# Attention probabilities turned by VectorE in 32x32 blocks and moved through DRAM instead of by TensorE

## The chip, the cores and the metric

The kernel runs on one core of one Trainium2 chip. The metric is the device time in microseconds (us) of the whole kernel, the median of several executions. The engines are TensorE (PE), VectorE (DVE), ScalarE (ACT), GpSimd (POOL) and SyncE (SP); SP, POOL and ACT issue the transfers, which 16 DMA engines carry out.

## What is computed

Two layers over 256 latent tokens and 256 context tokens of width 1024, all in float32. Cut to what matters here, a layer is

```
h, hc = modulate(rms_norm(x)), modulate(rms_norm(ctx))         # adaLN
a_b, a_c, a_x, na_q, na_k, na_v, sw_q, sw_k, sw_v, gates = split(h @ w_in)
o_a  = a_b * short_conv(a_c * a_x)                             # branch 0
o_na = neighbourhood_attention(na_q, na_k, na_v, context k, v, bias)   # branch 1, 8 heads of 64
o_sw = window_attention(sw_q, sw_k, sw_v, context k, v, sink)          # branch 2, 8 heads of 64
merged = sum_i sigmoid(gate_i) * (o_i @ w_branch[i])
x += gate * (merged @ w_out)
x += gate * expert_choice_ffn(h2)     # 16 experts, 1024 x 1024 gate, up, down
```

An attention is `softmax(q k^T + bias) v` over 512 keys (latent and context) for a latent query and over 256 context keys for a context query. The second layer has latent queries only, because the context is not needed after it.

## The kernel before

`make_plan` writes one list of steps for all engines; each engine walks the list and takes the steps that concern it, so that every engine's order is that list's order and semaphores tie the engines together. Around the attention the list is made of **pairs**. A pair is the two heads of one head pair `p` (0 to 3) for one tile of 128 queries. In layer one each `p` has four pairs: latent queries tile 0 (512 keys), context tile 0 (256 keys), latent tile 1, context tile 1. In layer two it has two, both with 512 keys. Over the two branches that is 32 pairs in layer one and 16 in layer two. A **set** is the pairs of one `p` that share a product with the values: two pairs.

`attention(br, p, info, fill)` places for each pair: the step `score` (TensorE makes both heads' scores into two PSUM banks, VectorE adds the bias and finds the maximum, ScalarE writes `PB = exp(scores)`), then a share of the filling blocks (`fill`: the products of the next `p`'s queries and keys, of gates and branches), and among them `normalise` for each head (VectorE: `PB *= 1/sum`, L1758). Behind the share stands `turn`: TensorE transposes each 128x128 piece of `PB` into a PSUM bank (L2058), ScalarE copies the bank to `PTL` or `PTC` (L1452). The step `pv` of a set (TensorE, L2071) stands in the next pair's filling; `o_low` follows it. So queries' probabilities are used as the moving operand of the value product about a third of a pair after they were turned.

A filling block is the product of a 128-column weight block with `HH`/`HL` or `OH`/`OL`, three matmuls for each of its 8 (or 4) row tiles (L2019 to L2021, "k steps"). Its weights come by SP's queue into a stretch of `ring` (`P.load`, two slots of 4096 words in layer one and three in layer two, used round and round), ScalarE rounds them to `WH` (L1362) and VectorE writes the rest `WL` (L1598), two blocks ahead of TensorE, with three buffers.

POOL serves the bias of the neighbourhood attention: for each unit (one head of one pair) two transfers from DRAM into `BIAS` (L1256) and an addition of the mask (L1227). SP waits at the step `gt2_bias` for the last value product of the layer (`pv_ready`) before it issues what stands behind it, the next dense weights and, in layer two, the first expert weights. The mixture of experts behind it streams 16 experts' weights through the ring.

## Time and profile before

| | us |
|---|---|
| median of 3 executions | 1842.83 (1837.32 to 1845.15) |
| the profiled execution, its own time | 1841.04 |
| its span in the profile | 1838.9 |
| TensorE, VectorE, ScalarE, GpSimd busy | 1690.3, 771.2, 478.1, 111.1 |

In the profiled execution layer one's attention lies from about 150 to 412 us, its experts from about 590 to 1070 us, layer two's attention from about 1123 to 1306 us, its experts from about 1396 us to the end. Times of instructions are read from such a profile with `PE` for matmuls and `PEld` for loads of the stationary operand; matmuls overlap, so that the distance between starts, and not the duration of one, is what one costs in a row of them.

### The profile page before, as it was taken

The numbers are of one execution on the slowest core, as the hardware profiler recorded it, in microseconds if no ns is written. First come the engines' busy times: TensorE is split into PE (matmuls) and PEld (weight loads), VectorE is DVE, ScalarE is ACT, GpSimd is POOL, SyncE is SP. The second block draws the span as 40 slices with busy tenths as digits, with TensorE's granted clock in tenths as the row PEclk, the third lists the DMA queues.
The fourth block names the chain that finished last, engine by engine and source line by source line (L and its number), as shares of the span: only waits on it lengthen the run. The fifth ranks groups of instructions, "written<-read, shape, count | busy, mean of one in ns | idle before, by whom it ended". The sixth has DMA issues, their size and how long they took to land.

```text
span 1838.9 us, 26514 instructions
## 1 busy us (share of the span) xinstructions
PE 1690.3 (92%) x10854; PEld 979.8 (53%) x10854; DVE 771.2 (42%) x1746; ACT 478.1 (26%) x1052; POOL 111.1 (6%) x149
## 2 busy tenths in 40 slices
PE   6999999999998999999988799989998998777876
PEld 3887777776664333333232498877882332222222
DVE  4455566665424233332323665577753222111111
ACT  4224455552132100000000434465441000000001
POOL 1012210000001000000000102300001000000000
PEclk9999999999998999999999899999999999999899
DMA  9353231127778999999999764337899999999997
GB/s 352 112 137 95 84 92 58 36 80 264 268 275 343 410 428 426 428 428 427 427 428 427 264 203 141 89 115 256 282 365 383 426 427 426 426 426 426 425 426 298
DMA packets 152035, 543.83 MB, mean 296 GB/s; under 512 B 10026, under 2 KB 92400, under 8 KB 126700
## 3 DMA queue, kind: packets, MB, share of 16 engines
q1 hardware_dynamic: 149104, 535.35, 74.2%
q0 software_dynamic: 2400, 6.16, 1.3%
q8 instruction: 87, 1.43, 0.3%
q10 hardware_dynamic: 412, 0.64, 0.1%
q14 instruction: 32, 0.26, 0.0%
HBM read 539.13 MB, written 2.98 MB: 295 GB/s over the span
## 4 chain that ended last, share of the span: by engine, by line
PE 69%; DMA 23%; DVE 4%; ACT 2%; issue 1%; SPq 1%; POOL 0%; DVEq 0%; ACTq 0%
PE bank L2158 20%; PE bank L2019 12%; PE bank L2020 11%; PE bank L2021 11%; DMA ring<-in_w_exp_down 8%; DMA ring<-in_w_exp_gate 7%; DMA ring<-in_w_exp_up 5%; DMA spare<-in_w_exp_gate 3%; PE bank L1934 2%; PE bank L2132 2%; PE bank L2048 2%; PE bank L2071 2%; PE bank L2058 2%; PE bank L2187 1%; DMA ring<-in_w_in 1%
## 5 line engine op out<-in xcount | busy, mean ns | idle before, releaser
L2158 PE MATMUL bank<-ring,XEP 128*32 128x256 f32 (+1 forms) x2384 | 385.3, 618 | 30.5 <-DMA ring<-in_w_exp_gate 15.2
L2019 PE MATMUL bank<-HH,WH 128*128 128x512 f32 (+1 forms) x864 | 312.2, 361 | 4.2 <-DVE HL L1627 3.1
L2020 PE MATMUL bank<-HL,WH 128*128 128x512 f32 (+1 forms) x864 | 300.5, 348 | 0.0
L2021 PE MATMUL bank<-HH,WL 128*128 128x512 f32 (+1 forms) x864 | 300.0, 347 | 0.0
L2158 PEld LDWEIGHTS bank<-ring,XEP 128*32 128x32 f32 (+1 forms) x2384 | 114.4, 130 | 271.2 <-issue 228.4
L1598 DVE TENSOR_TENSOR WL<-ring,WH 128x1024 fp32r<-128x1024 f32 (+1 forms) x172 | 185.2, 1079 | 133.6 <-ACT WH L1362 132.9
L1856 DVE TENSOR_TENSOR X<-X,bank 128x512 f32<-128x512 f32 x184 | 114.0, 682 | 186.5 <-PE bank L2187 99.4
L2019 PEld LDWEIGHTS bank<-HH,WH 128*128 128x128 f32 x864 | 164.0, 190 | 52.1 <-issue 24.5
L1362 ACT CAST WH<-ring 128x1024 fp32r<-128x1024 f32 (+1 forms) x172 | 158.1, 927 | 101.2 <-PE bank L2021 64.7
L2158 PE MATMUL bank<-ring,HIDT 128*32 128x256 f32 (+1 forms) x1232 | 151.6, 474 | 32.1 <-DMA ring<-in_w_exp_down 32.1
L2021 PEld LDWEIGHTS bank<-HH,WL 128*128 128x128 f32 x864 | 164.0, 190 | 21.0
L2020 PEld LDWEIGHTS bank<-HL,WH 128*128 128x128 f32 x864 | 164.3, 190 | 18.2
L2158 PEld LDWEIGHTS bank<-ring,HIDT 128*32 128x32 f32 (+1 forms) x1232 | 55.9, 123 | 110.8 <-issue 72.9
L1506 ACT ACTIVATE HIDT<-bank 128x512 f32<-128x512 f32 (+1 forms) x32 | 15.7, 490 | 371.7 <-PE bank L2220 371.7
L1891 DVE TENSOR_TENSOR HID<-TH,bank 128x512 f32<-128x512 f32 (+1 forms) x32 | 17.8, 555 | 211.7 <-issue 203.5
L1842 DVE TENSOR_TENSOR YE<-bank,GT 128x512 f32<-128x512 f32 (+1 forms) x32 | 17.9, 558 | 207.0 <-PE bank L2158 207.0
L1500 ACT ACTIVATE TH<-bank 128x512 f32<-128x512 f32 (+1 forms) x32 | 15.7, 490 | 284.3 <-PE bank L2158 284.3
L2019 PE MATMUL bank<-OH,WH 128*128 128x512 f32 (+1 forms) x192 | 67.8, 353 | 1.6 <-issue 0.8
L1284 POOL TENSOR_TENSOR XEP<-XEP,MOD 128x512 f32<-128x512 f32 (+1 forms) x32 | 25.8, 828 | 664.8 <-DVE XEP L1834 664.8
L2020 PE MATMUL bank<-OL,WH 128*128 128x512 f32 (+1 forms) x192 | 64.9, 338 | 0.0
L2021 PE MATMUL bank<-OH,WL 128*128 128x512 f32 (+1 forms) x192 | 64.7, 337 | 0.0
L1256 POOL DMA_DIRECT2D BIAS<-rpb_tiled x64 | 39.4, 620 | 327.0 <-DVE SM L1734 204.2
(244 smaller groups left out, 1961.5 us busy)
## 6 DMA issues: line engine op xcount, KB each, us to landing
ring<-in_w_exp_gate SPq DMA_DIRECT2D x55, 2048.0 KB, 31.1
ring<-in_w_exp_up SPq DMA_DIRECT2D x49, 2048.0 KB, 33.9
ring<-in_w_exp_down SPq DMA_DIRECT2D x48, 2048.0 KB, 35.7
ring<-in_w_ada SPq DMA_DIRECT2D x48, 1024.0 KB, 7.6
ring<-in_w_in SPq DMA_DIRECT2D x40, 1024.0 KB, 6.2
split_slot<-in_w_exp_up SPq DMA_DIRECT2D x8, 2048.0 KB, 28.9
split_slot<-in_w_exp_down SPq DMA_DIRECT2D x8, 2048.0 KB, 33.3
ring<-in_w_in SPq DMA_DIRECT2D x28, 512.0 KB, 5.4
```

Source lines behind the costliest of these rows:

```text
L1256: pool.dma_start(BIAS[x.at][64 * rr:64 * rr + 64, :].rearrange("p (r k) -> p r k", r=4), toeplitz).then_inc(bias_in[x.bias % 2], 16)
L1362: nc.scalar.copy(WH[b.buffer][:, 0:b.kk, :], w).then_inc(split_hi, 1)
L1598: nc.vector.tensor_tensor(WL[b.buffer][:, 0:b.kk, :], w, WH[b.buffer][:, 0:b.kk, :].bitcast(f32), ALU.subtract).then_inc(split_lo, 1)
L1856: nc.vector.tensor_tensor(xs, xs, ys, ALU.add).then_inc(x_added, 1)
L1934: last = mm(t[32 * j:32 * j + 32, :], CS[:, 4 * kk + j, :], w[:, j, :], start=kk == 0, stop=kk == 1, tile_position=(0, 32 * j))
L2019: mm(t, wh, hi[:, k, 0:b.n], start=k == 0, stop=False)
L2020: mm(t, wh, lo[:, k, 0:b.n], start=False, stop=False)
L2021: last = mm(t, wl, hi[:, k, 0:b.n], start=False, stop=k == b.kk - 1)
L2048: last = mm(SB_[x.u % 2][:, 0:x.nk], QS[x.p % 2][rows, qp, q0:q0 + 128], k, start=i == 0, stop=i == 2, tile_position=(64 * x.hh, 0))
L2058: last = nc.tensor.transpose(TB[x.u % 2][:, 128 * c:128 * c + 128], PB[x.u % 2][:, 128 * c:128 * c + 128], IDENT)
L2071: last = mm(PVB[64 * hh:64 * hh + 64, 0:SEQ], v, buf[:, hh, c, :], start=c == 0, stop=c == n - 1, tile_position=(0, 64 * hh))
L2158: last = mm(out_bank[tw * g:tw * g + tw, 0:nw], stationary(k), w[:, g::G] if spread else w[:, nw * g:nw * g + nw], start=k == 0, stop=k == ...
```

## The change

VectorE transposes each unit's `PB` in 32x32 blocks into `PBT`, right behind its normalisation. When both heads of a pair are there, POOL writes `PBT` to one of three DRAM tensors (`bounce`), and with four transfers reads it back so that block (i, j) lands at (j, i) in `PTL` or `PTC`. TensorE's transposes and ScalarE's copies are gone. In layer one the read-back is issued behind the next pair's write; in layer two right behind its own. The value product of a set is placed three pairs (layer one) or two pairs (layer two) behind the pair that ends it. `PBT` takes the last 1024 words of the streaming stretch of `ring` (`P.kept`). The bias transfers are placed by `bias_order` behind a pair's write, the two masks behind the four transfers. `gates_first` puts two gate blocks ahead of the branch blocks where a branch's values come late. The last sets of a layer are multiplied inside the first filling of branch 2.

```diff
@@ class Plan.load
-            if self.top + size > STREAM[self.layer] * SLOT:
+            if self.top + size > STREAM[self.layer] * SLOT - self.kept:
@@ attention
-                at_ = sorted(at_ + [(-(-per * 3 // 10), values), (-(-per * 7 // 10), lower)], key=lambda a: a[0])
+                at_ = sorted(at_ + [(-(-per * ((1 if br == 'sw' and p == 0 else 5) if last else 4) // 10), lambda: values(pair[0].pair - (2 if last else 3))), (-(-per * ((4 if br == 'sw' and p == 0 else 10) if last else 8) // 10), lower)], key=lambda a: a[0])
-        def values():
-
-            for st in P.turned:
-                P.add("pv", set=st)
-            P.lower += P.turned
-            P.turned = []
+        def values(until):
+
+            while P.turned and P.turned[0].end <= until + 1:
+                P.add("pv", set=P.turned[0])
+                P.lower.append(P.turned.pop(0))
@@ def turn(pair)
-            for x in pair:
-                P.add("turn", unit=x)
-                if x.end:
-                    P.turned.append(x.set)
+            P.add("turn", pair=pair)
+            P.fetches.append(pair)
+            if last or len(P.fetches) > 1:
+                P.add("fetch", pair=P.fetches.pop(0))
+            if pair[1].end:
+                P.turned.append(pair[1].set)
@@ branch 2, the first filling
+            if d2 == 0:
+                mid = 2 * KD + 3
+                atoms = gates_first(atoms)
+                done = 0
+                for n in (KD + 1, 2 * KD)[-len(P.turned):]:
+                    run(atoms[done:n])
+                    values(P.turned[0].end - 1)
+                    run(atoms[n:n + 3])
+                    lower()
+                    done = n + 3
+                run(atoms[done:mid])
@@ gpsimd
+                    elif s.kind == "turn":
+                        x = s.pair[1]
+                        pool.wait_ge(turn_ready, x.u + 1)
+                        run, held = 16 * x.nk // 32, bounce[x.pair % 3]
+                        if x.pair > 2:
+                            pool.wait_ge(pt_in[x.pair % 3], 64 * (x.pair // 3))
+                        pool.dma_start(held[:, 0:4 * run], PBT[l][x.set.grp][:].rearrange("p b h c j -> p (b h c j)")).then_inc(pt_out, 16)
+                    elif s.kind == "fetch":
+                        x = s.pair[1]
+                        run, held = 16 * x.nk // 32, bounce[x.pair % 3]
+                        pool.wait_ge(pt_out, 16 * (x.pair + 1))
+                        if x.set.pt_before:
+                            pool.wait_ge(pv_ready, x.set.pt_before)
+                        j = x.qt % 2
+                        for b in range(4):
+                            blocks = bass.AP(tensor=held.tensor, offset=held.offset + run * b, ap=[[PBT_W, 32], [32 * PBT_W, 4], [1, run]])
+                            turned = (PTL, PTC)[x.set.grp][32 * b:32 * b + 32, 4 * j:4 * j + 4].rearrange("p a h c j -> p a (h c j)")
+                            pool.dma_start(turned, blocks).then_inc(pt_in[x.pair % 3], 16)
@@ scalar, kind == "turn": the copy is gone
-                        nc.scalar.copy(buf[:, x.hh, :, 128 * j:128 * j + 128],
-                                       TB[x.u % 2][:, 0:128 * nk].rearrange("p (k q) -> p k q", k=nk)).then_inc(pt_ready, 1)
@@ vector, kind == "normalise"
+                        dve.wait_ge(norm_ready, x.u + 1)
+                        if x.hh == 0 and x.pair:
+                            dve.wait_ge(pt_out, 16 * x.pair)
+                        turned = PBT[l][x.set.grp][:, :, x.hh, :, :].rearrange("p b c j -> p c b j")
+                        nc.vector.transpose(turned, PB[u2][:, 0:n].rearrange("p (c b j) -> p c b j", b=4, j=32)).then_inc(turn_ready, 1)
@@ tensor, kind == "turn": the transposes are gone
-                        for c in range(x.nk // 128):
-                            last = nc.tensor.transpose(TB[x.u % 2][:, 128 * c:128 * c + 128], PB[x.u % 2][:, 128 * c:128 * c + 128], IDENT)
@@ tensor, kind == "pv"
-                        pe.wait_ge(pt_ready, st.end)
+                        for n in st.pairs:
+                            pe.wait_ge(pt_in[n % 3], 64 * (n // 3 + 1))
```

VectorE, first pair of layer one, before: the two heads' normalisations stand one behind the other, then a weight block's `WL`.

```order
L1750 TENSOR_TENSOR SM<-SM 128x1 [waits exp_ready]
L1757 RECIPROCAL SM<-SM 128x1 [waits dve_chain]
L1758 TENSOR_SCALAR PB_90<-PB_90,SM 128x512 [waits dve_chain]
...
L1758 TENSOR_SCALAR PB_91<-PB_91,SM 128x512 [waits dve_chain]
L1598 TENSOR_TENSOR WL_83<-ring,WH_80 128x1024 [waits split_hi]
```

The same place of the changed kernel:

```order
L1804 TENSOR_SCALAR PB_94<-PB_94,SM 128x512 [waits dve_chain]
L1809 STREAM_TRANSPOSE PBT_90<-PB_94 128x4x4x32 [waits norm_ready]
...
L1804 TENSOR_SCALAR PB_95<-PB_95,SM 128x512 [waits dve_chain]
L1809 STREAM_TRANSPOSE PBT_90<-PB_95 128x4x4x32 [waits norm_ready]
L1650 TENSOR_TENSOR WL_83<-ring,WH_80 128x1024 [waits split_hi]
```

A transpose of the unit's whole width stands behind each normalisation, 96 in the program, and `WL` stands behind both. From the second pair on the first of a pair's two also waits for `pt_out`, the pair before's write.

POOL, two pairs in the middle of layer one's neighbourhood attention, before: two units' bias transfers and masks.

```order
L1256 DMA BIAS_98<-rpb_tiled 64x4x64 [waits max_ready]
L1256 DMA BIAS_98<-rpb_tiled 64x4x64
L1227 TENSOR_TENSOR BIAS_98<-BIAS_98,CONST 128x256 [waits bias_in1]
L1256 DMA BIAS_97<-rpb_tiled 64x4x64 [waits max_ready]
L1256 DMA BIAS_97<-rpb_tiled 64x4x64
L1227 TENSOR_TENSOR BIAS_97<-BIAS_97,CONST 128x256 [waits bias_in0]
```

The same two pairs of the changed kernel:

```order
L1315 DMA bounce<-PBT_90 128x1024 [waits pt_in0,turn_ready]
L1305 DMA BIAS_102<-rpb_tiled 64x4x64 [waits max_ready]
L1305 DMA BIAS_102<-rpb_tiled 64x4x64
L1305 DMA BIAS_101<-rpb_tiled 64x4x64 [waits max_ready]
L1305 DMA BIAS_101<-rpb_tiled 64x4x64
L1276 TENSOR_TENSOR BIAS_102<-BIAS_102,CONST 128x256 [waits bias_in1]
L1276 TENSOR_TENSOR BIAS_101<-BIAS_101,CONST 128x256 [waits bias_in0]
L1326 DMA PTC<-bounce 32x4x128 [waits pv_ready,pt_out]
L1326 DMA PTC<-bounce 32x4x128 x3
L1315 DMA bounce<-PBT_91 128x512 [waits pt_in1,turn_ready]
L1326 DMA PTL<-bounce 32x4x256 [waits pv_ready,pt_out]
L1326 DMA PTL<-bounce 32x4x256 x3
```

Ten transfers (two writes, eight reads) have joined the four of the bias, in one queue, in order.

TensorE at the end of layer two's attention, before: the last pair's transposes (L2058), four k steps of branch 2's first gate block, then the last set's value product (L2071).

```order
L2021 MATMUL bank<-OH_60,WL_84 128x256
L2058 MATMUL bank<-CONST,PB_90 128x128 x4
L2058 MATMUL bank<-CONST,PB_91 128x128 x4
L2019 MATMUL bank<-HH,WH_82 128x256
L2020 MATMUL bank<-HL,WH_82 128x256
L2021 MATMUL bank<-HH,WL_85 128x256
...
L2071 MATMUL bank<-PTL,VS 64x256 x8
```

The same product in the changed kernel stands behind 13 k steps of branch 2, of which these are the last two, and three k steps ahead of a modulation product:

```order
L2070 MATMUL bank<-HH,WH_80 128x256
L2071 MATMUL bank<-HL,WH_80 128x256
L2072 MATMUL bank<-HH,WL_83 128x256
L2070 MATMUL bank<-HH,WH_80 128x256
L2071 MATMUL bank<-HL,WH_80 128x256
L2072 MATMUL bank<-HH,WL_83 128x256
L2115 MATMUL bank<-PTL,VS 64x256 x8
L2070 MATMUL bank<-HH,WH_80 128x256
```

From the last pair's scores to it the changed order has 25 k steps, another set's value product and one group of transposes of a modulation.

## Rows read from the trace of the kernel before

**Rows 1.** The page: busy time of each engine, and what the DMA engines moved by slice

```profile
PE 1690.3 (92%) x10854; PEld 979.8 (53%) x10854; DVE 771.2 (42%) x1746; ACT 478.1 (26%) x1052; POOL 111.1 (6%) x149
GB/s 352 112 137 95 84 92 58 36 80 264 268 275 343 410 428 426 428 428 427 427 428 427 264 203 141 89 115 256 282 365 383 426 427 426 426 426 426 425 426 298
```

**Rows 2.** Busy time by stretch: stretch, length, engines, clock, DMA share, GB/s

```profile
152.40:289.60 137.20, 137.20 (x716) 105.04 (x714) 77.86 (x213) 67.42 (x167) 23.73 (x37) 1.00 0.29 85
291.00:387.30 96.30, 96.30 (x513) 72.50 (x512) 64.20 (x190) 52.56 (x154) 0.00 (x0) 1.00 0.16 50
387.30:412.00 24.70, 24.70 (x137) 18.17 (x137) 18.70 (x58) 15.30 (x48) 0.00 (x0) 1.00 0.25 86
1123.10:1222.60 99.50, 93.39 (x650) 79.73 (x650) 65.21 (x165) 55.04 (x129) 24.47 (x36) 1.00 0.39 116
1222.60:1296.70 74.10, 74.10 (x591) 58.26 (x590) 56.78 (x162) 42.22 (x118) 0.00 (x0) 1.00 0.63 210
1440.00:1450.00 10.00, 10.00 (x84) 3.08 (x80) 2.28 (x6) 0.97 (x2) 0.00 (x0) 1.00 1.01 428
```

**Rows 3.** Chain of work through layer two's neighbourhood attention, 1186 to 1232 us

```profile
1190.78 0.95 ACT WH L1362
1191.75 1.23 DVE WL L1598
```

**Rows 4.** TensorE in order of time: two matmuls of a k step, and one turn

```profile
1239.73 0.28 PE L2019 MATMUL bank<-HH,WH 128*128 128x256 f32 x1
1239.85 0.28 PE L2020 MATMUL bank<-HL,WH 128*128 128x256 f32 x1
...
1241.96 1.04 PE L2058 MATMUL bank<-CONST,PB 128*128 128x128 f32 x8
1242.93 0.96 PE L2048 MATMUL bank<-dup,QS 64*128 64x512 f32 x6
```

**Rows 5.** The group of the transposes, whole span: busy, mean ns, idle before and its releaser

```profile
L2058 PE MATMUL bank<-CONST,PB 128*128 128x128 f32 x320 | 44.0, 274 | 4.3 <-DVE PB L1758 4.1
```

**Rows 6.** TensorE's waits from 1120 to 1330 us: total, times, longest

```profile
PE bank L2058 <- DVE PB L1758: 4.1, 5, 1.5
```

**Rows 7.** VectorE in order of time, layer two's windowed attention

```profile
1246.64 0.49 DVE L1758 TENSOR_SCALAR PB<-PB,SM 128x512 f32<-128x512 f32 x1
1248.18 0.68 DVE L1598 TENSOR_TENSOR WL<-ring,WH 128x512 fp32r<-128x512 f32 x1
...
1301.44 0.49 DVE L1758 TENSOR_SCALAR PB<-PB,SM 128x512 f32<-128x512 f32 x1
```

**Rows 8.** Groups of VectorE from 1222.6 to 1296.7 us, with idle before them

```profile
L1731 DVE CUSTOM_DVE_ANT_0 PB<-bank,CONST,SINK 128x256 f32<-128x256 f32 x14 | 6.8, 484 | 4.4 <-PE bank L2048 4.4
...
L1752 DVE TENSOR_REDUCE SM<-SM 128x1 f32<-128x3 f32 x14 | 2.1, 153 | 2.3 <-ACT SM L1443 2.3
```

**Rows 9.** POOL's transfers and masks: duration ns min/median/max

```profile
L1256 POOL DMA_DIRECT2D BIAS<-rpb_tiled x64: 615/615/667, 101.8 to 1191.6; - x64
L1227 POOL TENSOR_TENSOR BIAS<-BIAS,CONST x32: 725/740/1674, 107.0 to 1194.0; 128x256 f32<-128x256 f32 x32
```

**Rows 10.** Transfers: queue, count, KB each, median us from issue to landing

```profile
BIAS<-rpb_tiled POOLq DMA_DIRECT2D x64, 64.0 KB, 2.5
ring<-in_w_branch SPq DMA_DIRECT2D x24, 512.0 KB, 6.3
rpb_tiled<-RPBT POOLq DMA_DIRECT2D x2, 944.5 KB, 8.3
out<-XN SPq DMA_DIRECT2D x1, 512.0 KB, 3.8
```

**Rows 11.** Chain at layer two's last pair: its scores, the last value product

```profile
1296.67 0.94 PE bank L2048 x6
...
1306.29 1.88 PE bank L2071 x16
```

**Rows 12.** SP's queue from 1225 to 1480 us: who waited for whom

```profile
SPq L1193 <- PE bank L2071: 11.4, 1, 11.4
```

More of the change, by code:

```diff
@@ L161, in __init__ @@
         self.pair = pair
+        self.pairs = pairs
         self.parts = parts
@@ L829, in make_plan, with bias_order, pair @@
                 split(ahead[layer_blocks[1].b])
-        P.steps[l] = out
+        P.steps[l] = bias_order(out, 2 * (l + 1))
     return P
+def bias_order(steps, ahead):
+    due = [s for s in steps if s.kind == "bias"]
+    out = []
+    def pair():
+        now = [due.pop(0) for _ in range(2)] if due else []
+        out.extend(now + [Step(kind="mask", layer=s.layer, unit=s.unit) for s in now])
+    for s in steps:
+        if s.kind == "bias":
+            if s.unit.u == min(t.unit.u for t in steps if t.kind == "bias"):
+                for _ in range(ahead // 2):
+                    pair()
+            continue
+        out.append(s)
+        if s.kind == "turn" and s.pair[0].bias:
+            pair()
+    assert not due
+    return out
 def hybrid_dit_kernel(nc, A, out):
```

76 lines of the change are left out of this document (31 added, 45 removed).

## Prediction, made before the changed kernel ran

> **What bounds the kernel now.** First the page: TensorE is busy 92% of the span, VectorE 42% [rows 1]. A share of the whole says little here, so next the busy time by stretch. In layer one's attention TensorE has no idle time at all, and VectorE is at 57% in the neighbourhood part and 67% in the windowed part [rows 2]. In layer two the blocks are half as wide while the softmax of a pair stays: TensorE is busy 93.39 of 99.50 us in the neighbourhood part and all of the windowed part's 74.10, VectorE 65.21 and 56.78 of them, 77% in the latter [rows 2]. Third the chain of work: it is TensorE through layer one, but between about 1187 and 1222 us it goes again and again through ScalarE's rounding of a weight block and VectorE's remainder of it, 0.95 and 1.23 us, before TensorE can go on [rows 3]. So layer one's attention is TensorE's alone, layer two's is nearly shared with VectorE. Behind the attention the experts are bound by their weights: 428 GB/s, the most that any slice of the page shows [rows 1, 2]. That stream is released by steps at the end of the dense part, so what the dense part gains or loses moves it and the end one to one.
>
> **TensorE's transposes, removed.** 320 of them (192 in layer one, 128 in layer two). Eight stand from 1241.96 to 1242.93, that is 0.97 us or 0.121 each [rows 4]; the group's busy 44.0 us gives 0.138, but its first overlaps what stands ahead [rows 5]. At 0.121 it is 23.2 us in layer one and 15.5 in layer two. TensorE also waited 4.1 us for normalised probabilities in this group, all of it in layer two's attention [rows 5, 6]; that wait has no successor at this place, since the value product now comes two or three pairs later. Upper end of the gain: 38.7 + 4.1 = 42.8 us. ScalarE's copies go too; it is not the bound in these stretches, and I count nothing.
>
> **VectorE's transposes, added.** 64 of 512 columns and 32 of 256; before has none. Below: a normalisation of 512 columns takes 0.49 us. Above: if a column took twice as long as in a subtraction with 512 columns (0.68), the price would be near that of 1024 columns, 1.23 [rows 7]. I take the subtraction, 0.69 and 0.42 for 256 columns, because it takes one element at a time where the normalisation seems to take two. The Trainium skill ("VectorE: DVE Perf Modes", The three transpose paths) gives 311 ns for 128x128 of two-byte elements; worked on at one element a cycle that is an estimate of 0.71 us, and the sum would stay. The trace has no transpose by VectorE to check it.
>
> In layer one, 16 pairs at 1.38 and 16 at 0.84 us add 35.5 us. Two parts have room: the neighbourhood part goes to about 78 + 18 of 125 us, and the windowed part's first 12 pairs to 64 + 13 of 87; for VectorE's work then arriving late now and then I take 1.0 us off. Its last four pairs, with little filling, have 18.7 us of VectorE in 24.7; plus 4.4 it is 23.1, against 24.7 - 2.9 = 21.8 of TensorE [rows 2]. With a microsecond of waits that remain, they lose 2.3 of their gain.
>
> In layer two's windowed part seven pairs take 74.1 us with 56.8 of VectorE. Fourteen transposes add 9.7. Waits that its order keeps are for scores 4.4 and for ScalarE's sums 2.3 [rows 8]: 73.2 together, against 74.1 - 6.8 = 67.3 for TensorE. VectorE is the bound, and of 6.8 us 0.9 is left: a loss of 5.9, over eight pairs 6.7. In the neighbourhood part VectorE has 8.2 us in a pair of 12.4 and most pairs keep their 0.97; the three on the chain of [rows 3] keep none, a loss of 3.0.
>
> **The way through DRAM, added.** POOL gets five transfers a pair, 240 in all. One of its own takes 0.615 us to issue, lands 2.5 us later and is never slower than 0.667 [rows 9, 10]. 512 KB written to DRAM landed in 3.8 us from SP's queue, 944.5 KB in 8.3 from POOL's; 512 KB read in 6.3 [rows 10]. I take 0.615 per issue, 3.8 for a write, 2.5 for each read (128 KB) and up to 6.3 as the worse end. Two pairs of layer one's neighbourhood part have 14 issues and two masks, 8.6 + 1.5 us and some 2 for landing, in about 16 us: POOL keeps up. A write and its read-back, about 13 us with all issues, are hidden under two or three pairs of 8 us and more. The moved traffic, about 40 MB in all, meets DMA shares of 0.16 to 0.63 [rows 2]. VectorE's new wait (`pt_out`) is for a write issued most of a pair earlier: nothing. The ring's lost 1024 words leave layer one's loads at nearly the same places; nothing.
>
> **What is late next: the last sets.** In layer two POOL cannot read back pair 47's first neighbour, pair 46, before the set ahead is multiplied, some 5 us after pair 47's scores start (scores 0.94, six k steps at 0.36, the product 1.88 [rows 4, 11]). Then four issues to 7.5, pair 47's write issued by 8.1 and landed at 11.9, four more issues to 14.4, landed at 16.9. TensorE arrives after 25 k steps (9.0), scores, one product and eight transposes of a modulation: 0.9 + 9.0 + 1.9 + 1.0 = 12.8. It waits 4.2 us. VectorE is not the late one: its second normalisation ended 5.3 us after the scores' start [rows 7, 11], 6.7 with transposes. SP stands behind the same product (it waited 11.4 us for it before [rows 12]); the weights behind it have about two fillings of room. In layer one the same sum gives about 1.5 us.
>
> **Sum.** Layer one 23.2 - 1.0 - 2.3 - 1.5 = 18.4. Layer two 15.5 + 4.1 - 6.7 - 3.0 - 4.2 = 5.7. Together 24.1 us. From the profiled execution's own 1841.0 (2.2 beyond its span) that gives 1816.9; the median shown is 1.8 above it, so 1819.
>
> **Rivals.** (a) VectorE costs nothing more anywhere, since its waits shrink as ScalarE's copies go: 42.8 less 5.7 at the ends is 37, so 1806. For it speaks VectorE's idle time of 17 us in layer two's windowed part [rows 2]; against it that TensorE would need VectorE at nearly 100%.
>
> (b) The transposes are dear, 1.23 us (0.72 for 256 columns): 44 us more of VectorE in all. In layer two's windowed part that is 14 x 0.54 = 7.6 us for seven pairs, all on the bound, 8.6 for eight; in the neighbourhood part some 5 (3.3 of it in the three pairs on the chain); in layer one 3.5 in the last four pairs and some 5 in the twelve ahead of them, whose VectorE then has 64 + 23 of 87 us. Of the 24.1 about 2 are left: 1841, no change. The Trainium skill's rule in "VectorE: DVE Perf Modes" (Rules for kernel authors) to use TensorE for a 128x128 transpose whose target may be PSUM speaks the same way.
>
> (c) Slower: POOL becomes the bound. Two pairs of layer one's neighbourhood part leave 16 - 3.5 us for 14 issues, so from 0.9 us an issue on POOL decides, `pt_out` comes late, VectorE stops in front of its next transpose and TensorE for `WL`. At 1.5 us it is 8 times 8.5 = 68 us there and, with 18 issues in about 22 us, 4 times 8 = 32 in layer two's: a net loss of some 76, so 1919; at 1.1 us 28 are lost, a little more than the gain. Against it stands the even 615 ns of 64 issues amid a busy VectorE, while POOL's masks do stretch, to 1.67 us [rows 9]. The Trainium skill ("SBUF — State Buffer", the "DVE blocks DMA" trap) says that a POOL transfer's issue is shut out while VectorE runs an instruction on both SBUF ports, 620 ns becoming 3100. This trace's issues don't show it.
>
> **How the numbers follow.** The case of the sum 0.50 (1811 to 1828), (a) 0.20, (b) 0.18, (c) 0.12. Rival (a) reaches to about 1802, (b) to 1845; leaving out (c) and the outer parts of both the range is 1803 to 1841. About 0.5%, 9 us, is what a measurement of this kernel can tell from no change. Faster by more: 0.50, 0.20 and a third of (b), 0.76. Within: 0.10, half of (b) with a little of (c). Slower: 0.14.
>
> **What would show it.** The transposes' mean near 0.69 us; TensorE without idle time in layer one up to 400 us, with idle time behind VectorE's `WL` in layer two's windowed part; a wait of 3 to 6 us for `PTL` at layer two's last value product; POOL's issues at 0.6 us. Wrong would make it: transposes over 1 us, a stretched issue, waits of VectorE for `pt_out`, or value products that wait in the middle of the attention.

## The result, and the profile after

The changed kernel takes 1874.96 us (1873.06 to 1877.51), the kernel before 1841.44 in the same comparison: a ratio of 1.0187 (1.0175 to 1.0199), some 34 us slower where the prediction said 22 us faster. The profiled execution took 1873.06 us, its span is 1871.3.

The page, busy time by engine and the DMA queues (packets, MB, share of 16 engines' span); it answers to [rows 1]:

```profile
PE 1672.4 (89%) x10534; PEld 955.6 (51%) x10534; DVE 818.3 (44%) x1842; ACT 433.7 (23%) x956; POOL 243.4 (13%) x389
q0 software_dynamic: 16480, 48.12, 8.9%
```

TensorE does 18 us less and the span is 32 us longer: it waits. The first question is where. Busy time by stretch, columns as in [rows 2]; the stretches are layer one's attention up to its last scores, layer two's neighbourhood part, its windowed part to the last scores, and from there to its last value product:

```profile
142.60:393.10 250.50, 244.47 (x1194) 179.47 (x1193) 194.66 (x528) 111.72 (x310) 109.21 (x189) 0.99 0.60 172
1119.10:1227.50 108.40, 89.92 (x587) 76.35 (x586) 73.02 (x179) 46.84 (x114) 44.16 (x72) 0.91 0.62 177
1227.50:1310.70 83.20, 72.22 (x519) 56.15 (x518) 60.63 (x166) 34.57 (x103) 16.83 (x31) 0.90 0.77 243
1310.70:1335.70 25.00, 13.68 (x109) 11.82 (x106) 15.79 (x41) 6.30 (x17) 7.66 (x14) 0.96 0.94 296
```

Up to layer one's last scores the change works: they start at 393.1 us, before at 406.7. In layer two TensorE is idle for 41 of 217 us, and the granted clock is 0.90 to 0.96 where it was 1.00 [rows 2]. The lower clock costs time beside the waits: TensorE is busy 175.8 us in these three stretches, and in a kernel with the same order and no turning at all (`no turning` in the table below, granted clock 0.98) 166.9 us for the same matmuls. VectorE isn't full either (60.6 of 83.2), so it is not the bound that the prediction expected there.

The second question is what it waits for. Waits of TensorE from 1120 to 1400 us (total, times, longest), then POOL's from 1119 to 1336 us:

```profile
PE bank L2115 <- issue: 20.9, 4, 7.5
PE bank L2088 <- ACT QT L1471: 8.1, 3, 5.5
PE bank L2038 <- DVE MB L1654: 4.3, 1, 4.3
PE bank L2070 <- ACT GT L1476: 4.1, 1, 4.1
PE bank L2070 <- DVE WL L1650: 3.2, 1, 3.2
...
POOL PTL L1326 <- PE bank L2115: 48.0, 6, 11.3
POOL PTL L1326 <- DMA bounce<-PBT: 31.5, 5, 8.4
POOL BIAS L1276 <- DMA BIAS<-rpb_tiled: 26.8, 9, 6.9
```

L2115 is the value product. "issue" means that the profile shows no releaser, but the product waits for four reads of each of its set's two pairs. At the last product the chain counts 6.49 us of this wait from where a read of pair 46 landed; the product behind it takes 3.68 us, twice the 1.88 of [rows 11]:

```profile
1322.34 6.90 DMA PTL<-bounce
1329.24 6.49 issue
1335.73 3.68 PE bank L2115 x16
```

That read is not what the product waited for. Pair 47 was still on its way: POOL issued its write at 1322.88, stood 7.77 us until it had landed, and issued the read-back only at 1331.21. TensorE had been idle for 7.5 us in all when the product started, the longest wait of the list above:

```profile
1322.88 0.56 POOL L1315 DMA_DIRECT2D bounce<-PBT  x1
1331.21 2.18 POOL L1326 DMA_DIRECT2D PTL<-bounce  x4 [7.77 <-DMA bounce<-PBT]
```

The granted clock says why it takes twice as long. The stretch of the wait, then that of the product (0.50 is 1.2 of 2.4 GHz), and the 20 us around the same wait in layer one, 6.2 us from 402.8 us:

```profile
1330.00:1335.70 5.70, 0.00 (x0) 0.00 (x1) 0.00 (x0) 0.00 (x0) 2.18 (x4) 0.81 0.52 172
1335.70:1339.40 3.70, 3.67 (x17) 2.00 (x17) 0.00 (x0) 0.00 (x0) 0.00 (x0) 0.50 0.02 4
400.00:420.00 20.00, 13.75 (x69) 9.07 (x71) 2.40 (x5) 2.34 (x5) 3.11 (x6) 0.83 0.72 220
```

So such a wait is paid for once more in the product behind it. POOL in order of time shows how a product in the middle of the attention came late. Its wait lasts from 1154.54 to 1161.69 us:

```profile
1141.72 0.57 POOL L1315 DMA_DIRECT2D bounce<-PBT  x1
1142.29 2.45 POOL L1305 DMA_DIRECT2D BIAS<-rpb_tiled  x4
1151.63 2.41 POOL L1276 TENSOR_TENSOR BIAS<-BIAS,CONST 128x256 f32<-128x256 f32 x2 [6.89 <-DMA BIAS<-rpb_tiled]
1153.98 2.18 POOL L1326 DMA_DIRECT2D PTL<-bounce  x4
```

The pair was written at 1141.7. Behind the write stand the next biases and their masks; the masks wait 6.9 us for the biases to land, and only then, at 1154.0, is the pair read back: 12.3 us behind its write and 20 us ahead of the product (1141.7 to 1161.7). The landing itself is also longer than before. Transfers from 1119 to 1336 us (count, KB each, median us from issue to landing); in [rows 10] a bias took 2.5 and a branch's weights 6.3, and in layer two's attention alone, before, 2.9 and 6.0:

```profile
ring<-in_w_ada SPq DMA_DIRECT2D x12, 1024.0 KB, 8.4
bounce<-PBT POOLq DMA_DIRECT2D x16, 512.0 KB, 4.7
PTL<-bounce POOLq DMA_DIRECT2D x64, 128.0 KB, 3.1
ring<-in_w_in SPq DMA_DIRECT2D x8, 1024.0 KB, 8.9
ring<-in_w_branch SPq DMA_DIRECT2D x8, 512.0 KB, 10.6
...
BIAS<-rpb_tiled POOLq DMA_DIRECT2D x24, 64.0 KB, 6.2
```

Writes land late where the DMA engines are full. Of layer two's 16, eight landed in 3.0 to 4.3 us, with a DMA share of 0.54 to 0.92 while they were under way, and eight in 5.0 to 8.6 us, with 0.98 to 1.07. The stretches of one early write and of the last one (the DMA share is the last but one number):

```profile
1130.12:1133.20 3.08, 3.08 (x25) 2.54 (x25) 2.86 (x9) 0.92 (x3) 3.03 (x5) 1.00 0.54 192
1322.90:1330.90 8.00, 5.29 (x42) 4.88 (x41) 5.00 (x15) 1.51 (x3) 0.54 (x1) 1.00 1.06 318
```

Last the tile `PBT` over the whole span, VectorE's transposes and POOL's writes: duration min, median, max in ns, what the two waited for ahead of them, and the write's landing min, median, max:

```profile
L1809 DVE STREAM_TRANSPOSE PBT<-PB x96: 445/711/715, 146.6 to 1321.3; 128x512 f32<-128x512 f32 x64, 128x256 f32<-128x256 f32 x32
L1315 POOL DMA_DIRECT2D bounce<-PBT x48: 558/561/783, 149.1 to 1322.9; - x48
...
  DMA bounce<-PBT: 26.7, 12
...
DMA to landing us min/median/max: 2.3/3.6/8.6
```

VectorE's transposes cost what was predicted (0.69 taken, 0.711 measured). VectorE's wait for `pt_out` (the write before), costed at nothing, is 26.7 us over both layers.

### The profile page after: what moved, and what is told of

Read it like the earlier page. It is cut to its first block, busy times and chain, and to the rows that moved or that the text cites. A ratio compares the mean times of both kernels' runs of the same rounds, so it can differ in the third digit from the quotient of the medians.

```text
span 1871.3 us, 26051 instructions
## 1 busy us (share of the span) xinstructions
PE 1672.4 (89%) x10534; PEld 955.6 (51%) x10534; DVE 818.3 (44%) x1842; ACT 433.7 (23%) x956; POOL 243.4 (13%) x389
## 4 chain that ended last, share of the span: by engine, by line
PE 65%; DMA 24%; DVE 5%; issue 3%; ACT 2%; SPq 1%; POOL 0%; DVEq 0%; ACTq 0%; POOLq 0%
PE bank L2202 20%; PE bank L2070 11%; PE bank L2071 10%; PE bank L2072 10%; DMA ring<-in_w_exp_down 8%; DMA ring<-in_w_exp_up 7%; DMA ring<-in_w_exp_gate 4%; DMA spare<-in_w_exp_gate 2%; PE bank L2115 2%; PE bank L2176 2%; PE bank L1985 2%; PE bank L2099 2%; DMA ring<-in_w_in 1%; PE bank L2231 1%; DVE WL L1650 1%
## 5 line engine op out<-in xcount | busy, mean ns | idle before, releaser
L2071 PE MATMUL bank<-HL,WH 128*128 128x512 f32 (+1 forms) x864 | 302.2, 350 | 0.0
L2072 PEld LDWEIGHTS bank<-HH,WL 128*128 128x128 f32 x864 | 165.8, 192 | 20.9
L2071 PEld LDWEIGHTS bank<-HL,WH 128*128 128x128 f32 x864 | 166.3, 192 | 18.2
L1345 POOL TENSOR_TENSOR XEP<-XEP,MOD 128x512 f32<-128x512 f32 (+1 forms) x32 | 25.8, 828 | 668.3 <-DVE XEP L1885 668.3
L1326 POOL DMA_DIRECT2D PTL<-bounce x128 | 69.9, 553 | 81.5 <-PE bank L2115 48.0
L1809 DVE STREAM_TRANSPOSE PBT<-PB 128x512 f32<-128x512 f32 (+1 forms) x96 | 59.8, 623 | 29.6 <-DMA bounce<-PBT 26.7
L2071 PE MATMUL bank<-OL,WH 128*128 128x512 f32 (+1 forms) x192 | 65.1, 339 | 0.0
```

Of the source, the lines that this page charges most:

```text
L1326: pool.dma_start(turned, blocks).then_inc(pt_in[x.pair % 3], 16)
L1809: nc.vector.transpose(turned, PB[u2][:, 0:n].rearrange("p (c b j) -> p c b j", b=4, j=32)).then_inc(turn_ready, 1)
L2071: mm(t, wh, lo[:, k, 0:b.n], start=False, stop=False)
L2072: last = mm(t, wl, hi[:, k, 0:b.n], start=False, stop=k == b.kk - 1)
```

## The experiments

Each time is a median, beside the kernel before in the same comparison (1840 to 1842 us), with the ratio and its 95% interval. A table worked out from the traces stands behind them; its rows are called the table.

### What each part costs: leaving out the turning, the transposes, the waits

Three kernels go from nothing to nearly the whole change. In all three the products read `HH` and not the probabilities.

```diff
-                        for n in st.pairs:
-                            pe.wait_ge(pt_in[n % 3], 64 * (n // 3 + 1))
...
-                        buf, n = (PTL, 4) if st.grp == 0 else (PTC, 2)
+                        n = 4 if st.grp == 0 else 2
+                        buf = HH[:, 0:n, :].bitcast(f32).rearrange("p k (a h c j) -> p (k a) h c j", h=2, c=n, j=32)
```

In the first two POOL's steps `turn` and `fetch` are gone, and in the first VectorE's part of `normalise` too:

```diff
-                        turned = PBT[l][x.set.grp][:, :, x.hh, :, :].rearrange("p b c j -> p c b j")
-                        nc.vector.transpose(turned, PB[u2][:, 0:n].rearrange("p (c b j) -> p c b j", b=4, j=32)).then_inc(turn_ready, 1)
```

> The changed kernel without VectorE's transposes and without POOL's 240 transfers; the value products read a piece of HH in place of the probabilities, so the output of the attention branches is another. Nothing of the change but the removal of TensorE's transposes is left. All theories expect the upper end of the gain, 1841 - 42.8 = 1798 us (1790 to 1808). If it were above 1825, TensorE's transposes would have been hidden in the first place.

> The kernel above with VectorE's 96 transposes back in their places, but no transfer (the value products read a piece of HH, so the output is another). Theory A (the loss comes from the way through DRAM: the value products of layer two wait for a write and a read-back that stand behind one another in POOL's queue): 1811 us, the forecast's sum without its waits at the last sets, 1802 to 1822. Theory B (VectorE's 60 us of transposes are what is lost): 1850 or more.

> The changed kernel with all its transfers, but only the value products of each layer's last sets wait for them; the others read a piece of HH (the output is another), and the read-backs do not wait for a product. Theory A (waits in the chain product, read-back, write, read-back): the traffic alone costs little, so within 8 us of the kernel with no transfers, 1825 at most. Theory C (contention: 48 MB of small packets make the weights late): 1855 or more, most of the loss stays.

Measured: 1817.8 (ratio 0.9873, 0.9853 to 0.9892), 1826.4 (0.9921, 0.9905 to 0.9937) and 1857.5 us (1.0093, 1.0077 to 1.0109). The first missed by 20 us: removing TensorE's transposes, in this order of steps, gives 22 us and not 43. The second lies 8.6 us above it, which is what VectorE's transposes cost. It is 4 us above theory A's range, which was reckoned without the order's cost, and far below theory B's 1850: theory B is out. The transfers cost 31.0 us although only the last sets' products wait for them, and all other waits 17.5 more. The third, 1857.5, lies in the range of theory C and far above theory A's 1825. But VectorE and POOL still wait for writes in it (9.6 and 54.8 us in layer two), so it doesn't separate traffic from waits, and the next kernel has the transfers alone.

```diff
-                        pool.wait_ge(turn_ready, x.u + 1)
+                        pool.wait_ge(norm_ready, x.u + 1)
-                        pool.dma_start(held[:, 0:4 * run], PBT[l][x.set.grp][:]...).then_inc(pt_out, 16)
+                        pool.dma_start(held[:, 0:4 * run], HH[:, 0:2 * x.nk // 512, :]...).then_inc(pt_out, 16)
...
-                            turned = (PTL, PTC)[x.set.grp][32 * b:32 * b + 32, 4 * j:4 * j + 4]...
+                            turned = PBT[l][x.set.grp][32 * b:32 * b + 32]...
```

> The kernel without any turning (1817.8 us), with the changed kernel's 240 transfers of the same sizes and at the same places, issued by POOL when a pair is normalised, from a piece of HH and back into the place of PBT; no engine but POOL waits for them, apart from SP once a layer (the output is another, as there). Theory C (48 MB of transfers make the weights and biases land late): 1817.8 + 14 or more, 1832 to 1840. Theory A (only waits for the transfers cost): 1818 to 1823.

Measured: 1828.4 us (0.9935, 0.9920 to 0.9950), 10.6 above the kernel without them and between the two theories; about half of it stands behind the last product, where SP waits for these transfers in this kernel alone (the table, 539.1 against 533.2). Its transfers from 1106 to 1288 us land as late as in the changed kernel:

```profile
bounce<-HH POOLq DMA_DIRECT2D x16, 512.0 KB, 5.0
ring<-in_w_in SPq DMA_DIRECT2D x8, 1024.0 KB, 8.5
PBT<-bounce POOLq DMA_DIRECT2D x60, 128.0 KB, 4.0
ring<-in_w_branch SPq DMA_DIRECT2D x8, 512.0 KB, 9.9
```

but both layers' attention together is only 3 us longer. Weights that land late are hidden by the ring's room; traffic as such is the smaller part of the loss (10.6 us of the 49 that the transfers cost in the changed kernel), and theory C falls for most of it. What costs more is work that is tied to the transfers. The third kernel above has less of that than the changed kernel, yet it has the last sets' waits (6.8 and 8.1 us, with a lower clock behind them) and VectorE's for the write.

### The order without any turning

```diff
-                        for c in range(x.nk // 128):
-                            last = nc.tensor.transpose(TB[x.u % 2][:, 128 * c:128 * c + 128], PB[x.u % 2][:, 128 * c:128 * c + 128], IDENT)
```

> The kernel before with TensorE's transposes and ScalarE's copies left out and nothing else changed: its own order of steps, and value products that read a piece of HH (the output is another). It tells why the changed kernel's order without any turning gave 1817.8 us and not 1798. Theory D (the new order takes the rest: the last product stands 15 k steps later, gate blocks ahead of branch blocks): 1798 to 1806. Theory E (TensorE's removed time comes back as waits for the softmax and the rounding chain, whatever the order): 1813 to 1822.

The transposes and copies of the kernel before left out, and its value products read `HH`: 1805.1 us (0.9804, 0.9782 to 0.9826). So the removal is worth 35.7 us in the old order, and the new order alone takes 12.7 of it back. One more kernel moves the last sets' products, and with them branch 2's blocks, to their old places in the new order:

```diff
             if d2 == 0:
-                mid = 2 * KD + 3
-                atoms = gates_first(atoms)
-                done = 0
-                for n in (KD + 1, 2 * KD)[-len(P.turned):]:
...
+                run(atoms[:1 + KD // 2])
+                values(99)
+                run(atoms[1 + KD // 2:1 + KD])
+                lower()
+                run(atoms[1 + KD:mid])
```

> The changed kernel's order without any turning (1817.8 us), with the last sets' products of each layer where the kernel before has them, 4 k steps into branch 2, and branch 2's blocks in their old order. From the last product on, all kernels so far with the ring as in the changed kernel take 533 to 536 us to the end, wherever that product stands. Theory G (SP waits for that product before it issues what stands behind it, so the end follows the product, not TensorE's work): 6 to 10 us less, 1808 to 1812. Theory D2 (another part of the order, the gate blocks or the modulation product in the windowed part, takes the time): 1815 or more.

1812.4 us (0.9838, 0.9823 to 0.9853): 5.4 us of the 12.7, a little less than the 6 to 10 of theory G. The table bears it out: in the kernels with the ring as in the changed kernel, from the last product to the end it takes 533 to 536 us, whether 4 k steps of branch 2 stand ahead of it or 13. (That is 9 k steps in layer two, at 0.36 us the 3.3 us of the table; the 15 of the expectations were miscounted.) In the profiled executions 4.7 us of the gain lie in layer one and 3.3 in layer two, and 1.4 are lost behind them. The other 7 us lie in layer two, ahead of the last product (175.2 against 167.5): TensorE waits there 8.6 us for ScalarE's `QT`, in the old order 2.7. Which step of the order brings this was not tried. The changed kernel's wait for `QT` is as large (8.1 us), so it seems to come with the order and not with DRAM.

### One layer alone, and the last sets

The change in layer one, the kernel before in layer two; then layer one's last read-backs and products moved as well.

```diff
-            P.add("turn", pair=pair)
+            if last:
+                for x in pair:
+                    P.add("turn1", unit=x)
...
+            if pair[0].pair >= 30:
+                while P.fetches:
+                    P.add("fetch", pair=P.fetches.pop(0))
```

> The change in layer one alone; layer two's attention is that of the kernel before (TensorE's transposes, ScalarE's copies, its order). Layer one of the changed kernel reached layer two's first scores 3.9 us earlier than before (1119.1 against 1123.0). If the loss is made in layer two's attention alone: 1841 - 4 = 1837 us (1832 to 1841). If layer one's traffic or order costs something later that the trace does not show there: above 1845.

> As the kernel above, and layer one's last two read-backs stand right behind their own writes, its last two value products 12 and 15 k steps into branch 2 in place of 8 and 13. Theory A (what layer one's attention gains, 13.5 us at its last scores, is given back by the wait at the last sets' products, 6.3 us with a lower clock behind it): 5 to 8 us less than the kernel above, 1830 us. If the last sets wait for the transfers' landing under load wherever they stand, or something else holds layer one's end: no more than 2 us less.

1840.5 us (0.9995, 0.9985 to 1.0005) and 1841.9 us (1.0006, 0.9995 to 1.0017). The first was 3.5 above its expectation but says what it was to say: layer two costs the whole loss, and layer one gives nothing. The second missed its 1830: the wait at layer one's last products was spread and hardly shorter (6.9 us in two places before, 5.8 in three now). That the last pair's way through DRAM has its length wherever it is started fits this, but was not tried by itself. So the last pairs must not go that way:

```diff
-                        if l:
+                        if x.pair >= 28:
                             continue
                         dve.wait_ge(norm_ready, x.u + 1)
```

(against the kernel with layer one alone) and with it TensorE's transposes, ScalarE's copies and the places of products and blocks for pairs from 28 on, as in the kernel before.

> The change for the first 28 of layer one's 32 pairs alone; its last four pairs and layer two are turned by TensorE, with their products where the kernel before has them. Theory A (what layer one gains is given back at the last sets' products only): at pair 28 the kernel with layer one alone was 12.0 us ahead (375.2 against 387.2), and keeps it: 1841 - 12 = 1829 us (1826 to 1833). If it is lost elsewhere: 1838 or more.

1830.2 us (0.9942, 0.9925 to 0.9958), as expected: the last sets of layer one, in their new way and their new place together, cost 10.3 us. The place alone is a part of it, since the old place gave 4.7 us in layer one without any turning; the two were not separated here.

### What makes layer two's products late

First POOL's wait for the product ahead of a read-back, the largest in its list (48.0 us): a second buffer for every other set's first pair, in 1024 more words of the ring, and the product in two halves.

```diff
-        P.kept = PBT_W
+        P.kept = PBT_W * (2 if last else 1)
...
+                        if l and x.qt == 0:
+                            free = x.set.set - 1
+                        if free:
+                            pool.wait_ge(pv_ready, free)
```

> The changed kernel with a second buffer for the first pair of every other set in layer two (1024 words more taken from the weights' stretch of the ring), so that this read-back does not wait for the set before's value product; the product is made in two halves of 128 queries. Theory A: the waits of POOL for the product (48 us in 6) go, and with them most of the value products' waits: 1850 us or less (1835 to 1855). Theory C: 1870 to 1880, unchanged or a little worse for the shorter ring.

1875.9 us (1.0199, 1.0170 to 1.0227): no gain. POOL's waits for the product are gone from its list, but its waits for writes to land grew from 31.5 to 54.5 us in their place, and the value products still wait 18.3 us (20.9 before). Beside the kernel with two `PBT` below, which gives up as many words of the ring, it is 7.5 us faster: a small gain that the shorter ring takes back. Then read-backs behind the next pair's write, with the products later in the filling:

```diff
-            if last or len(P.fetches) > 1:
+            while len(P.fetches) > 1 or P.fetches and pair[0].pair in (39, 46, 47):
                 P.add("fetch", pair=P.fetches.pop(0))
```

> The changed kernel with layer two's read-backs issued behind the next pair's write, as in layer one (but for the last neighbourhood pair and the last two), and its value products at 8 tenths of the second pair's filling in place of 5. POOL then stands neither for a write to land nor for a product. Theory A (POOL's order of waits: 31.5 us for writes, 48 for products): the value products' 20.9 us of waits in layer two fall below 10 and the time to 1857 to 1866. Theory C (landing times under the added traffic set it): the products wait for the reads as before, 1870 or more.

1882.6 us (1.0228, 1.0213 to 1.0243), 8 us worse: the products waited 25.8 us and not 20.9. POOL waited less for products (18.9 us) and writes (7.0), as much for biases (24.8), and the data came a pair later. Then a second `PBT`, so that VectorE doesn't wait for a write:

```diff
-                            dve.wait_ge(pt_out, 16 * x.pair)
+                            dve.wait_ge(pt_out, 16 * (x.pair - (x.pair > 33)))
```

> The changed kernel with two PBT in turn in layer two (1024 words more of the ring), so that VectorE's next transposes never wait for a write to land. Theory F (VectorE, stopped in front of its transposes with WL and the next softmax queued behind, is what makes layer two slow): its 8.7 us of waits there go and the time falls to 1860 to 1868. Theory A (the value products' waits for the way through DRAM decide): 1872 or more, as the products wait as before.

1883.4 us (1.0231, 1.0216 to 1.0246), 8 us above the changed kernel, and not the 1860 to 1868 of theory F. VectorE's waits for writes in layer two are gone from its list, and the attention is as long as before (215.1 against 216.6 us in the table). The value products waited as before (21.3 us). Theory F is out. What this kernel lost it lost behind the last product (546.7 against 535.6), as did all with a shorter ring in layer two. So the ring was measured by itself, and the products' place against it:

```diff
-            if self.top + size > STREAM[self.layer] * SLOT:
+            if self.top + size > STREAM[self.layer] * SLOT - self.kept:
```

> The kernel before with 1024 words less of the ring's stretch from the values' product to the last loads of the dense part, as in the changed kernel; nothing else. The forecast costed this at nothing: 1839 to 1843. Theory H (two kernels with 2048 words less in layer two took 9 to 11 us more behind the last product, so a shorter ring makes weights late): 1846 or more.

```diff
-        P.kept = PBT_W
+        P.kept = PBT_W * (3 if last else 1)
```

> The changed kernel with 2048 words less of layer two's ring and nothing else. Theory H: 1885 to 1895. If the ring is of no account: 1875.

```diff
+        PTL2 = [PTL, sb("PTL2", [128, 8, 2, 4, 32], R_RING + 16384 * STREAM[1] - 12 * PBT_W)]
...
-lambda: values(pair[0].pair - (2 if last else 3))
+lambda: values(pair[0].pair - (2 if last and br == 'sw' and p == 0 else 3))
```

> The changed kernel with a whole second PTL in layer two (2048 words more of the ring) and its value products one pair later, 3 pairs behind the pair that ends a set (but for the last neighbourhood set). Against the next kernel, which gives up the same words alone. Theory A (the way through DRAM takes longer than two pairs, so that the product waits): the products' 21 us of waits fall to those of the two last sets (8 to 12), and the time by 10 to 15 us against the next kernel. If the products wait as before: no difference.

1024 words less in the kernel before: 1841.7 us (1.0003, 0.9992 to 1.0015), nothing, as forecast. 2048 more in layer two: 1887.0 us (1.0252, 1.0233 to 1.0271), 12 us. A second `PTL` and a pair's more room for the products, against that: 1882.1 us (1.0217, 1.0202 to 1.0232), 4.9 less, not the 10 to 15 expected. The value products' waits shrank to 5.0 us at one product, but with the shorter ring alone they were 12.0 already and not 21. The others stayed: a modulation product waits 7.9 us for ScalarE (10.7 with the shorter ring alone).

What none of these touched is the order of POOL's own work in the neighbourhood part. First in layer one, on top of the kernel with 28 pairs:

```diff
     def pair():
         now = [due.pop(0) for _ in range(2)] if due else []
-        out.extend(now + [Step(kind="mask", layer=s.layer, unit=s.unit) for s in now])
+        masks.extend(Step(kind="mask", layer=s.layer, unit=s.unit) for s in now)
+        out.extend(now)
...
+        if s.kind == "fetch":
+            out.extend(masks)
+            masks.clear()
```

> As h3 (first 28 pairs of layer one changed, 1830.2 us), with layer one's two masks behind the read-back's four transfers in POOL's queue in place of ahead of them. In h3 POOL waited 10 us for biases to land with the read-back queued behind (its masks 261 to 268 us, then the read-back, then a value product that waited 3.3 us and a VectorE that waited up to 4.0 for the next write). Theory A: 5.1 us of product waits and most of 13.1 us of VectorE's go, 1822 to 1827 us. If these waits cost nothing: 1830.

```diff
-                    late = {28: 8, 29: 5, 31: 3}.get(pair[0].pair, 4)
+                    late = {28: 8, 29: 5, 31: 3}.get(pair[0].pair, 6)
```

> As h4, with layer one's value products at 6 tenths of the filling in place of 4. If products still wait in h4, 1 to 3 us less than it; if not, the same within 1 us, or a little more because the next read-back of the same buffer waits for the product.

1823.8 us (0.9909, 0.9893 to 0.9924) and 1823.2 us (0.9901, 0.9883 to 0.9919). The order gives 6.5 us, as expected; the products' place nothing more. TensorE's waits from 150 to 430 us in the first, where the kernel with layer one alone had 12.3 us for products and the one with 28 pairs 5.1:

```profile
PE bank L2169 <- issue: 1.1, 2, 0.8
PE bank L2113 <- ACT GT L1505: 0.7, 1, 0.7
```

Then the same order in the whole changed kernel, both layers:

> The whole changed kernel (1875 us) with the masks behind the read-back in POOL's queue in both layers, as h4 has it in layer one. Theory A (POOL's order of waits, not the landing): layer one gives the 6.5 us that it gave there; in layer two POOL waited 26.8 us for biases ahead of read-backs, and with them first the products at 1154 and 1215 us, which waited 7.2 and 5.7 us, come nearly in time: 1853 to 1862. If layer two's products are late by the landing and the distance alone: 1868.

1859.1 us (1.0107, 1.0090 to 1.0124): in the expected range, 15.9 us less than the changed kernel, with nothing added or removed. POOL in order of time, the same place in the program as shown above:

```profile
1137.54 0.57 POOL L1324 DMA_DIRECT2D bounce<-PBT  x1 [2.27 <-DVE PBT L1818]
1138.11 2.46 POOL L1314 DMA_DIRECT2D BIAS<-rpb_tiled  x4
1141.70 2.18 POOL L1335 DMA_DIRECT2D PTL<-bounce  x4 [1.13 <-DMA bounce<-PBT]
1145.61 1.58 POOL L1285 TENSOR_TENSOR BIAS<-BIAS,CONST 128x256 f32<-128x256 f32 x2 [1.74 <-DMA BIAS<-rpb_tiled]
```

The read-back stands 4.2 us behind the write's issue, and not 12.3; the masks wait 1.74 us in its shadow. TensorE's and POOL's waits in layer two there:

```profile
PE bank L2124 <- issue: 9.5, 2, 8.8
...
POOL BIAS L1285 <- DMA BIAS<-rpb_tiled: 4.4, 4, 1.7
```

POOL's waits for biases fell from 26.8 to 4.4 us. The products in the middle are in time; of 9.5 us 8.8 stand at the last.

### The table

Profiled executions, us. Layer one is from its first scores to layer two's first scores, layer two from there to its last value product, the rest from there to the span's end; each the difference of two starts in the trace. A profiled execution can lie some us off the median: the second half buffer's took 1884.0 us (median 1875.9), the ring shorter by 2048's 1881.3 (1887.0), the others lie within 3.2 us of theirs.

| kernel | layer one | layer two | the rest |
|---|---|---|---|
| before | 980.4 | 183.2 | 532.7 |
| no turning, old order | 958.9 | 167.5 | 533.8 |
| no turning, last products early | 957.7 | 175.2 | 534.6 |
| no turning | 962.4 | 178.5 | 533.2 |
| no transfers | 958.8 | 188.7 | 533.0 |
| traffic alone | 962.1 | 181.7 | 539.1 |
| not waited for | 970.6 | 207.6 | 534.9 |
| changed | 976.5 | 216.6 | 535.6 |
| changed, masks behind | 971.0 | 207.3 | 534.9 |
| layer one alone | 977.8 | 183.3 | 535.4 |
| 28 pairs | 966.8 | 182.7 | 534.1 |
| 28 pairs, masks behind | 960.5 | 183.4 | 532.7 |
| layer one alone, last read-backs at once | 981.7 | 183.4 | 533.2 |
| read-backs deferred | 977.3 | 222.7 | 535.6 |
| second half buffer | 981.3 | 211.7 | 546.1 |
| two PBT | 977.0 | 215.1 | 546.7 |
| ring shorter by 2048 | 976.7 | 214.8 | 546.5 |
| the same, products later | 976.7 | 211.6 | 547.1 |

## Why the prediction was wrong

The prediction was wrong in sign: 1819 us forecast, 1874.96 measured, outside its range of 1803 to 1841. By its own steps:

- **What bounds the kernel now** was read rightly. That the end moves one to one with the dense part held too, with one thing missed: it moves with the last value product, since SP waits for it. "The weights behind it have about two fillings of room" was wrong. The last products' later place (with branch 2's blocks) cost 5.4 us, the new order in all 12.7, and the sum had nothing for it.
- **TensorE's transposes, removed.** Upper end 42.8 us, measured 35.7: near, 20 % too large.
- **VectorE's transposes, added.** 0.69 us taken, 0.711 measured; 13.0 us of lost gain forecast, 8.6 measured. In the profiled executions layer two lost 10.2 us by them (forecast 9.7), and layer one nothing (958.8 against 962.4, where 3.3 were forecast). Rivals (a) and (b) fell with it. The Trainium skill ("VectorE: DVE Perf Modes", The three transpose paths) had led to an estimate of 0.71 us, and the trace agrees.
- **The way through DRAM, added.** This is the step that failed: "A write and its read-back, about 13 us with all issues, are hidden under two or three pairs of 8 us and more". It priced POOL's work and not the order of POOL's waits. The pair shown above was 20 us on its way from its write to its product, which waited 7.15 us for it. In front of a read-back stand two masks that wait for biases, and those waits grew with the new traffic: in layer two a bias lands in 6.2 us (2.9 before, 3.5 in the new order without turning), and POOL stood 26.8 us for them (9.6 and 12.8). "POOL keeps up" took "some 2 for landing" in two pairs, and was worked out for layer one only. Moving the masks behind the read-back gave 15.9 us in the changed kernel and 6.5 in layer one's 28 pairs, so this cause is shown for these 16 us. All that the transfers cost, 1874.96 - 1826.4 = 49 us, stood in the sum with 5.7.
- **What is late next: the last sets.** The mechanism was right and its size too small. Forecast 1.5 us in layer one and 4.2 in layer two (its own terms give 4.1). In layer one the old way and place for these pairs gave 10.3 us: the waits (6.4 us at the first of them), the clock (in the changed kernel 0.83 from 400 to 420 us) and the place of the products. In layer two the last product waited 7.5 us and ran 1.8 us longer at half clock. Counted from the last pair's first scores (1310.7 us), the write was forecast at 8.1 and landed at 11.9, the read-back at 16.9; measured are 12.2, 20.2 and 25.0, with 8.0 us for the write where the sum had 3.8. The sum counted no clock.
- **`pt_out`**: "nothing" for 26.7 us of waits. With these gone in layer two (8.7 us) the attention was 215.1 us, with only the ring made shorter (by 2048 words) 214.8, so the cost is small there, though the reason given was wrong. **The ring's lost words**: nothing, measured nothing; 2048 more in layer two cost 12.
- **The rivals.** (c) had the right sign and the wrong mechanism. POOL's issues stayed at 0.55 to 0.62 us in the median, beside a busier VectorE. What came late was POOL's waits, a case that no rival held: the chance of slower was put on a stretched issue alone. The Trainium skill ("SBUF — State Buffer", the "DVE blocks DMA" trap and "A bandwidth-pool intuition that's wrong") has a POOL transfer grow from about 620 to about 3100 ns beside a VectorE copy, since its descriptors can't be written. This trace doesn't show it: no issue of this kernel's 240 took over 0.8 us.

What stays open: with the masks moved the whole change is still 32.7 us above the kernel without transfers (1859.1 against 1826.4). Layer one has 12 us of that and layer two 19 (the table). The last sets are a part of both, measured in layer one only. For the rest in layer two, late landings (a write 3.0 to 8.6 us, the long ones while the DMA engines were full), VectorE's and ScalarE's work queued behind late products, and the lower clock behind waits are candidates; no run takes one of them away by itself. Of the three single waits taken away, none gave more than 7.5 us even beside a kernel with as short a ring, and the runs don't divide it further.

## What to carry to other kernels

A detour over DRAM cost here by its latency in the queues that waited for it, and little by its issues. Write down, for the queue that carries it, each instruction in order with what it waits for, and put what only waits for itself behind what others wait for. That alone was worth 16 us here. Where a chain ends, at the last sets of a layer, little work is left to hide the latency: let those few go the old way (10.3 us in layer one, with their place). With 28 of layer one's 32 pairs on the new path and the masks behind the read-back the kernel takes 1823.8 us, 0.9909 (0.9893 to 0.9924) of the kernel before, and is faster than both.

A wait listed as large need not be worth much: when POOL's 48 us for the product went, its waits for writes grew by 23 us and TensorE's wait was nearly the same, and VectorE's 8.7 us went without gain. And a change that pays with buffer space needs the space alone as its comparison: 2048 words of the ring cost 12 us here. Leaving the work out step by step (no turning, transposes alone, transfers alone) told where the time was, which the list of waits could not.

## What the runs showed of the hardware

TensorE's granted clock was 0.50 behind 7.5 us without a matmul, and the product behind it took 3.68 us for 1.88. Half of layer two's 16 writes of 512 KB landed in 3.0 to 4.3 us, with the DMA engines at a share of 0.54 to 0.92 meanwhile, the other half in 5.0 to 8.6 us, with 0.98 to 1.07. The mean share of such a stage hides that (0.62 in the neighbourhood part). With 240 transfers and 42 MB more, transfers of other kinds landed later as well: in layer two's attention 512 KB of weights in 10.6 us for 6.0, 64 KB of bias in 6.2 for 2.9. A VectorE transpose of 128x512 float32 in 32x32 blocks took 0.711 to 0.715 us, of 256 columns 0.445 to 0.449.
